# Between the output projection and the feed-forward network: reordering ScalarE, VectorE and GpSimd around the last token tile

## Chip, cores and metric

The kernel runs on one core of one Trainium2 chip. The metric is the device time of one execution, in microseconds (us). Engines are named as in the profile: PE is TensorE, DVE is VectorE, ACT is ScalarE, POOL is GpSimd, SP is SyncE, which here only issues transfers.

## The reference, cut to what matters

One layer of a hybrid diffusion backbone over 1024 tokens of width 1024. The change touches only the seam between its two halves:

```python
    m = (g[:, :, 0] * (ya @ w_branch[0]) + g[:, :, 1] * (yb @ w_branch[1])
         + g[:, :, 2] * (yc @ w_branch[2]))
    return m @ w_out
...
        x = x + mod_x[2] * rms_norm(mix, norm_g[l, 1])
        h2 = modulate(x, norm_g[l, 2], mod_x[3], mod_x[4])
        x = x + mod_x[5] * rms_norm(swiglu(h2, w_ffn_in[l], w_ffn_out[l]), norm_g[l, 3])
```

## The kernel before

All large products are taken in three passes over operands cut in two: a high part in the format of the fast float32 product (a copy to fp32r) and a low part (the value minus its high part). `parts_product` (L78 to L80) multiplies high by high, high by low and low by high, so every operand must be cut first. ScalarE makes high parts, GpSimd or VectorE the low ones; a low part reads two tensors in SBUF.

`residual_ffn_in` does two things. First, for each of 8 tiles t of 128 tokens (the last is t = 7, `LAST`), the output projection of the merged branches, then the residual and the second norm. PE accumulates the tile in two banks of PSUM. ACT takes its sum of squares (`square`), DVE the mean, ACT the root, DVE the reciprocal and the product with gate row and root (L2657, `o_xn`), which frees the banks (`taken`), and adds it to x (L2660, `x_ready`). ACT takes the sum of squares of x (`square_x`), DVE scales it (L2668, `xn_ready`), PE turns the tile (`turn`, 8 transposes), and `modulate` applies scale and shift out of PSUM into `h2`, on ACT, for the last tile half on ACT and half on DVE (L2693).

Second, the input projection of the feed-forward network over 22 pairs of gate and up weights, as a block scheme with 7 products (0 to 6) per pair in place of 8, of 12 matmuls each. It needs sums of blocks: on the side of `h2` the `half_sums` (T1 and T3, two subtractions of 128x512 for a token tile), T2 (`second_sum`), T4 (`fourth_sum`); on the side of the weights `s13` (two sums), `s2` and `s4`. All of these read two tensors in SBUF. In the profile T1 and T3 parts are `m_parts`, T2, B22 and T4 parts `i_t_hi` and `i_t_lo`, the first half's parts `b_hi` and `b_lo`, weights and their parts `stage`, `i_raw`, `i_s` and `i_hi`, `i_lo`, `cut_hi`, `cut_lo`.

The seam is the stretch in which the last tile's chain meets the first pair's products. Nothing schedules it but the order written out by hand: each engine works through its list in order and waits at semaphores. PE's list there is: tile 7's projection, turn of tile 6, product (0,0) (product 0 of pair 0), product (3,0) into the same bank, turn of tile 7, product (0,1) of the next pair, then (1,0), (2,0), (4,0), (6,0), (5,0) and from there the pairs' regular steps from (1,1) on. Product (3,0) waits for ACT's copy of the bank (`t1_ready`, L2429), which itself waits for `taken`. Product (0,1) waits for its weight's low part by POOL (`weight_lo(1, 1, 0)`). Product (1,0) waits for T1's low part, (4,0) for T2's, and (1,1) for the next pair's sum `s13(1, 1)` (L2618, L2620) with its high and low part.

## Time and profile before

| | us |
|---|---|
| median of 3 runs | 1778.73 (1776.87 to 1779.0) |
| the profiled execution | 1778.41 |
| its span | 1776.4 |
| PE busy | 1737.5 (98%) |
| DVE busy | 1222.7 (69%) |
| ACT busy | 804.2 (45%) |
| POOL busy | 766.7 (43%) |

The profiled execution is 2.0 us longer than its span, since the span begins with the first instruction and ends with the last. The seam lies at 1120 to 1170 us of it. A share of busy time is an average over the whole kernel: in the seam PE waits, and there DVE's list is full.

### The profile page before, as it was taken

What the parts mean: (1) busy time and instruction counts of PE and PEld (TensorE: products, weight loads), DVE (VectorE), ACT (ScalarE), POOL (GpSimd) and SP (SyncE); (2) the same over time, 40 slices, a digit from 0 to 9 for tenths busy, and PEclk for the clock granted to TensorE, in tenths of its full rate; (3) what the DMA queues carried; (4) which work ended last, traced back from release to release, by engine and by line L of the source; (5) the groups of instructions that cost most, each with busy time, mean ns of one, the idle gap of its engine ahead of it and who ended that gap; (6) DMA issues with size and microseconds to landing.
All of it is one profiled execution on the core that took longest, in us unless ns stands there. A gap on an engine that the chain in (4) does not pass through costs nothing. (4 is left out here: it accounts for less than half of the span.)

```text
span 1776.4 us, 25757 instructions
## 1 busy us (share of the span) xinstructions
PE 1737.5 (98%) x9180; PEld 1479.4 (83%) x9180; DVE 1222.7 (69%) x1719; ACT 804.2 (45%) x1576; POOL 766.7 (43%) x494
## 2 busy tenths in 40 slices
...
GB/s 329 106 103 123 115 119 143 156 153 182 265 172 210 170 146 137 151 33 72 1 143 160 89 166 84 83 106 120 94 94 127 121 94 128 114 278 208 253 102 177
DMA packets 98375, 249.86 MB, mean 141 GB/s; under 512 B 12257, under 2 KB 25953, under 8 KB 98146
## 3 DMA queue, kind: packets, MB, share of 16 engines
...
## 5 line engine op out<-in xcount | busy, mean ns | idle before, releaser
L736 POOL TENSOR_TENSOR ring<-raw_w,ring 128x512 fp32r<-128x512 f32 x120 | 186.9, 1575 | 139.9 <-ACT ring L607 139.8
L78 PE MATMUL psum<-h_hi,ring 128*128 128x512 f32 x400 | 156.8, 392 | 3.0 <-ACT z L653 2.0
L80 PE MATMUL psum<-h_hi,ring 128*128 128x512 f32 x400 | 156.4, 391 | 0.0
L79 PE MATMUL psum<-h_lo,ring 128*128 128x512 f32 x400 | 156.2, 391 | 0.0
L78 PE MATMUL psum<-u_slot 128*128 128x512 f32 x308 | 120.5, 391 | 0.9 <-DVE u_slot L2933 0.7
L80 PE MATMUL psum<-u_slot 128*128 128x512 f32 x308 | 120.2, 390 | 0.0
L79 PE MATMUL psum<-u_slot 128*128 128x512 f32 x308 | 119.9, 389 | 0.0
L607 ACT ACTIVATE ring<-raw_w 128x512 fp32r<-128x512 f32 x120 | 72.5, 625 | 101.0 <-DVE raw_w L895 32.3
L1386 DVE TENSOR_REDUCE mx<-psum 128x1 f32<-128x1280 f32 x64 | 95.1, 1486 | 6.8 <-PE psum L1272 6.0
L1319 ACT ACTIVATE e<-psum,neg_m 128x1280 f32<-128x1280 f32 x64 | 85.0, 1328 | 31.2 <-DVE neg_m L1387 31.2
L2532 POOL TENSOR_TENSOR cut_lo<-i_raw,cut_hi 128x512 fp32r<-128x512 f32 x44 | 66.8, 1520 | 59.2 <-ACT cut_hi L2387 59.2
L78 PEld LDWEIGHTS psum<-h_hi,ring 128*128 128x128 f32 x400 | 75.5, 189 | 20.1 <-issue 4.0
L79 PEld LDWEIGHTS psum<-h_lo,ring 128*128 128x128 f32 x400 | 75.5, 189 | 15.7
L80 PEld LDWEIGHTS psum<-h_hi,ring 128*128 128x128 f32 x400 | 75.4, 189 | 15.8
L2532 POOL TENSOR_TENSOR cut_lo<-stage,cut_hi 128x512 fp32r<-128x512 f32 x40 | 59.9, 1498 | 64.0 <-ACT cut_hi L2387 64.0
L1271 PE MATMUL psum<-k_st,q_st 128*128 128x512 f32 (+1 forms) x192 | 74.2, 387 | 5.6 <-ACT e L1319 4.6
L1285 PE MATMUL psum<-val,at 128*128 128x128 f32 x640 | 76.7, 275 | 0.0
L1285 PEld LDWEIGHTS psum<-val,at 128*128 128x128 f32 x640 | 74.0, 192 | 0.0
L78 PE MATMUL psum<-b_hi,cut_hi 128*128 128x512 f32 x176 | 69.5, 395 | 4.4 <-ACT gate_row L2429 2.0
L78 PE MATMUL psum<-m_parts,i_hi 128*128 128x512 f32 x176 | 69.5, 395 | 1.1 <-issue 0.8
L1723 ACT ACTIVATE we<-psum,wneg_m 128x640 f32<-128x640 f32 (+1 forms) x64 | 49.1, 768 | 46.8 <-DVE wneg_m L1835 44.0
L78 PE MATMUL psum<-i_t_hi,cut_hi 128*128 128x512 f32 x176 | 68.6, 390 | 1.3 <-POOL i_lo L2532 1.3
...
## 6 DMA issues: line engine op xcount, KB each, us to landing
...
```

The source lines that it names most:

```text
L78: pe.matmul(out, sh, mh, start=first, stop=False, skip_group_check=onto)
L79: pe.matmul(out, sh, ml, start=False, stop=False, skip_group_check=onto)
L80: return pe.matmul(out, sl, mh, start=False, stop=last, skip_group_check=onto)
L607: act.activation(w_hi[i], source(p, i), ACT.Copy).then_inc(w_hi_ready, 1)
L736: pool.tensor_tensor(w_lo[i], source(p, i), w_hi[i].bitcast(F32), ALU.subtract).then_inc(w_lo_ready, 1)
L1271: pe.matmul(out, q, k_st[j][:, s, c0:c0 + w], start=True, stop=False)
L1285: mm = pe.matmul(bank[:, 2 * P:3 * P], at[t % 2][:, k, :], val[t // TL % 2][:, k, :], start=(k == 0), stop=(k == TT - 1))
L1319: act.activation(e[i % 2][s][:], psum[:, 3 * s * HALF:3 * s * HALF + TOK], ACT.Exp, scale=SCALE, bias=neg_m[:, i % 2, s:s + 1], accum_out= ...
L1386: ch.link(v.tensor_reduce(mx[:, s:s + 1], psum[:, 3 * s * HALF:3 * s * HALF + TOK], AX.X, ALU.max))
L1723: act.activation(e[u % 2][s][:, 0:keys], psum[:, 2 * s * HALF + CTX:2 * s * HALF + CTX + keys], ACT.Exp, scale=SCALE, bias=neg_m[:, u % 2, ...
L2532: pool.tensor_tensor(f_lo[i], source(q, i), f_hi[i].bitcast(F32), ALU.subtract).then_inc(fw_lo_ready, 1)
```

## The change

Only the seam is edited.

- ACT: the root of tile 7 comes behind two conversions of tile 6; the high parts of weights 4 and 5 come later; the conversions of tile 7 come directly behind those of tile 6; T1 and T3 of tiles 6 and 7 are cut together, 128x4x256 in place of two of 128x4x128.
- DVE: for tile 7 the product with the gate row (L2668 of the changed kernel) is taken before the root is waited for, and frees the banks; root and residual then make one instruction (L2674). `s2` goes behind `o_xn`, `s4` behind T4's sum; the low parts of weights 6, 4 and 5 leave, those of 1 and 2 go behind x. T1 and T3 sums and low parts of tiles 6 and 7 are one instruction of 128x4x256 each.
- POOL: it no longer waits for three low parts of weights before its two T1 and T3 low parts of tile 5 (`m_parts`), no longer sums tile 6, and takes the low parts of weights 6, 4 and 5, the first once x of tile 7 is there.
- SP's next weight transfer waits for the split semaphores in place of one.

```diff
@@ -2288,24 +2292,25 @@
             mm = product(0, 1)
-            pe.wait_ge(w0_lo, w0_at(1))
-            pe.wait_ge(part_lo, 2 * FH - 1)
+            pe.wait_ge(*w0_lo_of[1])
+            pe.wait_ge(part_lo, 5)
             pe.wait_ge(taken, TL)
             product(1, 0).then_inc(prod0, 1)
-            pe.wait_ge(w0_lo, w0_at(2))
-            pe.wait_ge(part_lo, 2 * FH)
+            pe.wait_ge(*w0_lo_of[2])
+            pe.wait_ge(part_lo, 6)
             product(2, 0).then_inc(prod0, 1)
-            pe.wait_ge(w0_lo, w0_at(4))
+            pe.wait_ge(*w0_lo_of[4])
             pe.wait_ge(t_lo_ready[T2], 1)
             product(4, 0, lambda k: pe.wait_ge(t2b_lo_ready, k // 2 + 1)).then_inc(prod0, 1)
             pe.sem_inc(prod_done, PRODUCTS + 1)
-            pe.wait_ge(full_ready, KC * TL)
+            pe.wait_ge(full_ready, KC * LAST + KC // 2)
+            pe.wait_ge(last_full, KC // 2)
...
-            def square(t):
                                accum_out=ss[:, t % 2, 0:1]).then_inc(ss_ready, 1)
+                between()
                 act.wait_ge(mean_ready, 2 * t + 1)
                 act.activation(rs[:, t % 2, 0:1], ss[:, t % 2, 0:1], ACT.Sqrt).then_inc(root_ready, 1)
@@ -2420,10 +2426,8 @@
             first_weight_hi(6)
             first_weight_hi(1)
             first_weight_hi(2)
-            square(LAST)
-            first_weight_hi(4)
-            first_weight_hi(5)
-            modulate(LAST - 1, 0, 5)
+            square(LAST, lambda: modulate(LAST - 1, 0, 2))
+            modulate(LAST - 1, 2, 5)
             act.wait_ge(prod0, prod0_at(0))
             act.wait_ge(taken, TL)
             act.activation(t1, banks[0], ACT.Copy).then_inc(t1_ready, 1)
@@ -2431,10 +2435,14 @@
             act.sem_inc(fw_hi_ready, PRODUCTS)
             weight_hi(1, 1, 0)
             modulate(LAST - 1, 5, KC)
-            t1_hi(LAST - 1)
+            modulate(LAST, 0, KC // 2)
+            act.wait_ge(last_sums, 1)
+            act.activation(t1_part[0][:, :, two_first], h2[:, 0:KH, two_first], ACT.Copy).then_inc(part_hi, 1)
+            act.wait_ge(last_sums, 2)
+            act.activation(t3_part[0][:, :, two_first], h2[:, 0:KH, two_second], ACT.Copy).then_inc(part_hi, 1)
+            first_weight_hi(4)
             act.wait_ge(t2_sum, 2)
             t_part_hi(T2, slice(0, KH), slice(0, HALF // 2))
...
@@ -2484,11 +2492,9 @@
                 weight_hi(p + 1, q + 1, 6)
 
             every, far = slice(0, KH), slice(HALF // 2, HALF)
-            modulate(LAST, 0, KC // 2)
-            t1_hi(LAST)
-            t3_hi(LAST)
             act.wait_ge(t2_sum, 3)
             t_part_hi(T2, every, far)
+            first_weight_hi(5)
             t_part_hi(B22, slice(0, 2), slice(0, HALF))
@@ -2523,9 +2529,6 @@
                 pool.wait_ge(sums_done, 2 * (t - FH) + 1)
                 pool.wait_ge(full_ready, KC * (t + 1))
                 nc.gpsimd.tensor_tensor(h2[:, 0:KH, b], h2[:, KH:KC, b], h2[:, 0:KH, b], ALU.subtract).then_inc(sums_done, 1)
-                if t == LAST - 1:
-                    pool.sem_inc(fw_lo_ready, PRODUCTS)
-                    weight_lo(1, 1, 0)
 
...
             half_sums(FH + 1)
-            pool.wait_ge(w0_lo, 3)
             pool.tensor_tensor(src[T2][:, :, near], h2[:, KH:KC, beyond], src[T2][:, :, near], ALU.subtract).then_inc(t2_sum, 1)
-            half_sums(FH + 2)
             pool.wait_ge(t2_sum, 2)
             pool.wait_ge(t4_sum, 1)
             pool.tensor_tensor(src[T4][:, :, near], src[T4][:, :, near], src[T2][:, :, near], ALU.subtract).then_inc(t4_sum, 1)
+            def first_weight_lo(i):
+                pool.wait_ge(w0_hi, w0_at(i))
+                pool.tensor_tensor(f_lo[i], source(0, i), f_hi[i].bitcast(F32), ALU.subtract).then_inc(w0_lo_pool, 1)
+
+            pool.wait_ge(chunk_done, 4)
+            pool.wait_ge(x_ready, TL)
+            first_weight_lo(6)
+            pool.sem_inc(fw_lo_ready, PRODUCTS)
+            weight_lo(1, 1, 0)
+            first_weight_lo(4)
+            first_weight_lo(5)
             for i in range(1, PRODUCTS):
...
@@ -2604,13 +2616,14 @@
 
             def first_weight_lo(i):
                 v.wait_ge(w0_hi, w0_at(i))
-                v.tensor_tensor(f_lo[i], source(0, i), f_hi[i].bitcast(F32), ALU.subtract).then_inc(w0_lo, 1)
+                v.tensor_tensor(f_lo[i], source(0, i), f_hi[i].bitcast(F32), ALU.subtract).then_inc(w0_lo_dve, 1)
 
             def s13(p, q):
                 gate, up = raw[q % 2]
                 v.wait_ge(i_in[q % 2], (p - q % 2) * 16 + 32)
                 if q == 1:
-                    v.wait_ge(w0_lo, w0_at(2))
+                    v.wait_ge(w0_lo_pool, 3)
+                    v.wait_ge(*w0_lo_of[2])
@@ -2649,17 +2662,24 @@
                 root = lambda i: rs[:, t % 2, i:i + 1]
                 v.wait_ge(ss_ready, 2 * t + 1)
                 v.tensor_scalar(ss[:, t % 2, 0:1], ss[:, t % 2, 0:1], 1.0 / D, EPS, ALU.mult, ALU.add).then_inc(mean_ready, 1)
+                if t:
+                    v.wait_ge(turned, t)
+                if t == LAST:
+                    ch.link(v.tensor_tensor(xn[:], acc, row[:], ALU.mult))
+                    v.sem_inc(taken, 1)
                 v.wait_ge(root_ready, 2 * t + 1)
                 ch.link(v.reciprocal(root(0), root(0)))
-                if t:
-                    v.wait_ge(turned, t)
-
-                ch.link(v.scalar_tensor_tensor(out=xn[:], in0=acc, scalar=root(0), in1=row[:], op0=ALU.mult, op1=ALU.mult))
-                v.sem_inc(taken, 1)
                 v.wait_ge(x_in[t % 2], 16 * (t // 2 + 1))
-                v.tensor_tensor(x[t % 2][:], x[t % 2][:], xn[:], ALU.add).then_inc(x_ready, 1)
                 if t == LAST:
-                    first_weight_lo(4)
+                    v.scalar_tensor_tensor(out=x[t % 2][:], in0=xn[:], scalar=root(0), in1=x[t % 2][:], op0=ALU.mult,
+                                           op1=ALU.add).then_inc(x_ready, 1)
+                    v.wait_ge(chunk_done, 4)
+                    first_weight_lo(1)
+                    first_weight_lo(2)
+                else:
+                    ch.link(v.scalar_tensor_tensor(out=xn[:], in0=acc, scalar=root(0), in1=row[:], op0=ALU.mult, op1=ALU.mult))
+                    v.sem_inc(taken, 1)
+                    v.tensor_tensor(x[t % 2][:], x[t % 2][:], xn[:], ALU.add).then_inc(x_ready, 1)
                 v.wait_ge(ss_ready, 2 * t + 2)
                 v.tensor_scalar(ss[:, t % 2, 1:2], ss[:, t % 2, 1:2], 1.0 / D, EPS, ALU.mult, ALU.add).then_inc(mean_ready, 1)
                 v.wait_ge(root_ready, 2 * t + 2)
@@ -2667,16 +2687,11 @@
                 v.wait_ge(x_ready, t + 1)
                 v.tensor_scalar(xn[:], x[t % 2][:], root(1), None, ALU.mult).then_inc(xn_ready, 1)
                 if t == LAST:
-                    first_weight_lo(5)
+                    s2(0, 0)
                 if 1 <= t <= FH:
                     h_parts(t - 1)
                 if t == LAST - 1:
                     s13(0, 0)
-                    s2(0, 0)
-                    s4(0, 0)
-                    v.wait_ge(chunk_done, 4)
-                    for i in W0[:3]:
-                        first_weight_lo(i)
                 if t == FH + 1:
                     for n in range(2):
 
             far, beyond = slice(HALF // 2, HALF), slice(SEQ - HALF // 2, SEQ)
-            v.wait_ge(part_lo, 4)
-            part_lower(LAST - 1, 0)
             v.wait_ge(turned, TL)
             for k in range(KC // 2, KC):
                 v.tensor_scalar(h2[:, k, LAST * P:TL * P], turned_x(LAST, k), A2[:, k:k + 1], B2[:, k:k + 1], ALU.mult,
-                                ALU.add).then_inc(full_ready, 1)
-            a, b = first_half(LAST), second_half(LAST)
-            v.wait_ge(full_ready, KC * TL)
-            v.wait_ge(sums_done, 2 * (FH - 1))
-            v.tensor_tensor(h2[:, 0:KH, a], h2[:, 0:KH, b], h2[:, 0:KH, a], ALU.subtract).then_inc(sums_done, 1)
-            v.wait_ge(sums_done, 2 * FH - 1)
-            v.tensor_tensor(h2[:, 0:KH, b], h2[:, KH:KC, b], h2[:, 0:KH, b], ALU.subtract).then_inc(sums_done, 1)
-            part_lower(LAST - 1, 1)
-            part_lower(LAST, 0)
-            part_lower(LAST, 1)
-            v.wait_ge(part_lo, 2 * FH - 1)
+                                ALU.add).then_inc(last_full, 1)
+            v.wait_ge(full_ready, KC * LAST + KC // 2)
+            v.wait_ge(last_full, KC // 2)
+            v.tensor_tensor(h2[:, 0:KH, two_first], h2[:, 0:KH, two_second], h2[:, 0:KH, two_first], ALU.subtract).then_inc(last_sums, 1)
+            v.wait_ge(last_sums, 1)
+            v.tensor_tensor(h2[:, 0:KH, two_second], h2[:, KH:KC, two_second], h2[:, 0:KH, two_second], ALU.subtract)\
+             .then_inc(last_sums, 1)
+            v.wait_ge(part_lo, 4)
+            for n, (part, whole) in enumerate(((t1_part, two_first), (t3_part, two_second))):
+                v.wait_ge(part_hi, 5 + n)
+                v.tensor_tensor(part[1][:, :, two_first], h2[:, 0:KH, whole], part[0][:, :, two_first].bitcast(F32), ALU.subtract)\
+                 .then_inc(part_lo, 1)
+            v.wait_ge(part_lo, 5)
             v.wait_ge(t2_sum, 2)
             second_sum(far, beyond, FH)
             v.wait_ge(t4_sum, 2)
             fourth_sum(far, FH - 1)
+            s4(0, 0)
             t_part_lo(T2, slice(0, KH), slice(0, HALF // 2), 1, t_lo_ready[T2])
             for n in range(2):
```

VectorE from behind tile 6's `o_xn` to tile 7's second mean, before the change (`stage` and `i_s` are weights and their sums, `o_ss` the sums of squares):

```order
L2618 TENSOR_TENSOR i_s<-stage 128x512
L2620 TENSOR_TENSOR stage<-stage 128x512
L2629 TENSOR_TENSOR stage<-stage 128x512
L2636 TENSOR_TENSOR stage<-stage 128x512
L2607 TENSOR_TENSOR i_lo<-stage,i_hi 128x512 x2
L2607 TENSOR_TENSOR i_lo<-i_s,i_hi 128x512
L2651 TENSOR_SCALAR o_ss<-o_ss 128x1
L2653 RECIPROCAL o_rs<-o_rs 128x1
L2657 SCALAR_TENSOR_TENSOR o_xn<-psum,o_rs,gate_row 128x1024
L2660 TENSOR_TENSOR o_x<-o_x,o_xn 128x1024
L2607 TENSOR_TENSOR cut_lo<-stage,cut_hi 128x512
L2664 TENSOR_SCALAR o_ss<-o_ss 128x1
```

and after it:

```order
L2631 TENSOR_TENSOR i_s<-stage 128x512
L2633 TENSOR_TENSOR stage<-stage 128x512
L2664 TENSOR_SCALAR o_ss<-o_ss 128x1
L2668 TENSOR_TENSOR o_xn<-psum,gate_row 128x1024
L2671 RECIPROCAL o_rs<-o_rs 128x1
L2674 SCALAR_TENSOR_TENSOR o_x<-o_xn,o_rs,o_x 128x1024
L2619 TENSOR_TENSOR i_lo<-stage,i_hi 128x512
L2619 TENSOR_TENSOR i_lo<-i_s,i_hi 128x512
L2684 TENSOR_SCALAR o_ss<-o_ss 128x1
```

The sums `s2` and `s4` and the low part of weight 6 have left the place ahead of the first mean, and the low parts of weights 1 and 2 have come between x and the second mean in place of that of weight 4.

VectorE from tile 7's `o_xn` to the first low part of T2, before:

```order
L2668 TENSOR_SCALAR o_xn<-o_x,o_rs 128x1024
L2607 TENSOR_TENSOR cut_lo<-stage,cut_hi 128x512
L2596 TENSOR_TENSOR m_parts<-h,m_parts 128x4x128
L2693 TENSOR_SCALAR h<-psum,A,B 128x128 x4
L2698 TENSOR_TENSOR h<-h 128x4x128
L2700 TENSOR_TENSOR h<-h 128x4x128
L2596 TENSOR_TENSOR m_parts<-h,m_parts 128x4x128 x3
L2599 TENSOR_TENSOR h<-h 128x4x256
L2603 TENSOR_TENSOR h<-h 128x4x256
L2710 TENSOR_TENSOR i_t_lo<-h,i_t_hi 128x4x256
```

and after:

```order
L2688 TENSOR_SCALAR o_xn<-o_x,o_rs 128x1024
L2642 TENSOR_TENSOR stage<-stage 128x512
L2706 TENSOR_SCALAR h<-psum,A,B 128x128 x4
L2710 TENSOR_TENSOR h<-h 128x4x256
L2712 TENSOR_TENSOR h<-h 128x4x256
L2717 TENSOR_TENSOR m_parts<-h,m_parts 128x4x256 x2
L2611 TENSOR_TENSOR h<-h 128x4x256
L2615 TENSOR_TENSOR h<-h 128x4x256
L2649 TENSOR_TENSOR stage<-stage 128x512
L2725 TENSOR_TENSOR i_t_lo<-h,i_t_hi 128x4x256
L2725 TENSOR_TENSOR i_t_lo<-h,i_t_hi 128x2x256 x2
```

Behind the four conversions `h<-psum,A,B` stand seven wide instructions and `s4` (the second `stage<-stage`) where five of 128x4x128 and three wide ones stood, counting up to the first low part of T2.

GpSimd from tile 5's sums to the first low part of the next pair's sums, before:

```order
L2522 TENSOR_TENSOR h<-h 128x4x128
L2525 TENSOR_TENSOR h<-h 128x4x128
L2568 TENSOR_TENSOR m_parts<-h,m_parts 128x4x128 x2
L2573 TENSOR_TENSOR h<-h 128x4x128
L2522 TENSOR_TENSOR h<-h 128x4x128
L2525 TENSOR_TENSOR h<-h 128x4x128
L2532 TENSOR_TENSOR cut_lo<-i_raw,cut_hi 128x512
L2577 TENSOR_TENSOR h<-h 128x4x128
L2532 TENSOR_TENSOR i_lo<-i_raw,i_hi 128x512
```

and after:

```order
L2528 TENSOR_TENSOR h<-h 128x4x128
L2531 TENSOR_TENSOR h<-h 128x4x128
L2570 TENSOR_TENSOR m_parts<-h,m_parts 128x4x128 x2
L2575 TENSOR_TENSOR h<-h 128x4x128
L2578 TENSOR_TENSOR h<-h 128x4x128
L2581 TENSOR_TENSOR i_lo<-stage,i_hi 128x512
L2535 TENSOR_TENSOR cut_lo<-i_raw,cut_hi 128x512
L2581 TENSOR_TENSOR cut_lo<-stage,cut_hi 128x512 x2
L2535 TENSOR_TENSOR i_lo<-i_raw,i_hi 128x512
```

The two sums of tile 6 are gone from it, and three low parts of weights of the first pair have come, two of them behind the low part of the next pair's weight 0.

## Rows read from the trace of the kernel before

**Rows 1.** The page of the profile: span, and the busy time of TensorE.
```profile
span 1776.4 us, 25757 instructions
PE 1737.5 (98%) x9180; PEld 1479.4 (83%) x9180; DVE 1222.7 (69%) x1719; ACT 804.2 (45%) x1576; POOL 766.7 (43%) x494
```

**Rows 2.** The timeline of PE at the seam: start us, us, what, idle before.
```profile
1127.17 0.39 PE L80 MATMUL psum<-b_hi,cut_lo 128*128 128x512 f32 x1
1129.61 0.50 PE L78 MATMUL psum<-b_hi,cut_hi 128*128 128x512 f32 x1 [2.05 <-ACT gate_row L2429]
...
1134.02 1.06 PE L2244 MATMUL psum<-ident,o_xn 128*128 128x128 f32 x8
1136.73 0.50 PE L78 MATMUL psum<-b_hi,cut_hi 128*128 128x512 f32 x1 [1.65 <-POOL cut_lo L2532]
...
1140.50 0.47 PE L78 MATMUL psum<-m_parts,i_hi 128*128 128x512 f32 x1 [0.77 <-issue]
...
1146.18 0.39 PE L78 MATMUL psum<-i_t_hi,cut_hi 128*128 128x512 f32 x1
...
1154.83 0.48 PE L78 MATMUL psum<-m_parts,i_hi 128*128 128x512 f32 x1 [0.30 <-POOL i_lo L2532]
...
1168.37 0.47 PE L78 MATMUL psum<-i_t_hi,cut_hi 128*128 128x512 f32 x1 [1.28 <-POOL i_lo L2532]
```

**Rows 3.** Stretches: us, busy PE PEld DVE ACT POOL, PE clock, DMA share, GB/s.
```profile
1130.50:1134.50 4.00, 4.00 (x15) 3.11 (x14) 3.45 (x6) 3.39 (x9) 3.08 (x3) 0.57 0.32 131
```

**Rows 4.** The timeline of VectorE (DVE) at the seam, columns as in Rows 2.
```profile
1121.97 0.69 DVE L2620 TENSOR_TENSOR stage<-stage 128x512 f32<-128x512 f32 x1
...
1126.51 1.28 DVE L2657 SCALAR_TENSOR_TENSOR o_xn<-psum,o_rs,gate_row 128x1024 f32<-128x1024 f32 x1
1127.94 1.93 DVE L2660 TENSOR_TENSOR o_x<-o_x,o_xn 128x1024 f32<-128x1024 f32 x1
1129.80 1.78 DVE L2607 TENSOR_TENSOR cut_lo<-stage,cut_hi 128x512 fp32r<-128x512 f32 x1
1131.50 0.14 DVE L2664 TENSOR_SCALAR o_ss<-o_ss 128x1 f32<-128x1 f32 x1
...
1132.11 1.16 DVE L2668 TENSOR_SCALAR o_xn<-o_x,o_rs 128x1024 f32<-128x1024 f32 x1
...
1135.48 1.36 DVE L2693 TENSOR_SCALAR h<-psum,A,B 128x128 f32<-128x128 f32 x4
1137.10 1.38 DVE L2698 TENSOR_TENSOR h<-h 128x512 f32<-128x512 f32 x1 [0.26 <-ACT h L2354]
...
1140.92 1.22 DVE L2599 TENSOR_TENSOR h<-h 128x1024 f32<-128x1024 f32 x1
...
1143.38 3.62 DVE L2710 TENSOR_TENSOR i_t_lo<-h,i_t_hi 128x1024 fp32r<-128x1024 f32 x5
...
1151.14 0.68 DVE L2618 TENSOR_TENSOR i_s<-i_raw 128x512 f32<-128x512 f32 x1
```

**Rows 5.** Groups of VectorE: line, shapes, count, busy us, mean ns, idle.
```profile
L3149 DVE SCALAR_TENSOR_TENSOR u_high<-u_high,u_ss,u_x 128x1024 f32<-128x1024 f32 x4 | 5.1, 1285 | 0.1
```

**Rows 6.** The timeline of GpSimd (POOL) at the seam, columns as in Rows 2.
```profile
1119.49 1.29 POOL L2525 TENSOR_TENSOR h<-h 128x512 f32<-128x512 f32 x1
1126.06 2.73 POOL L2568 TENSOR_TENSOR m_parts<-h,m_parts 128x512 fp32r<-128x512 f32 x2 [5.28 <-DVE i_lo L2607]
1128.73 2.30 POOL L2573 TENSOR_TENSOR h<-h 128x512 f32<-128x512 f32 x1
1130.99 1.73 POOL L2522 TENSOR_TENSOR h<-h 128x512 f32<-128x512 f32 x1
...
1136.64 1.28 POOL L2577 TENSOR_TENSOR h<-h 128x512 f32<-128x512 f32 x1
```

**Rows 7.** The timeline of ScalarE (ACT) before the last tile's square.
```profile
1122.69 0.64 ACT L2375 ACTIVATE i_hi<-stage 128x512 fp32r<-128x512 f32 x1 [0.72 <-DVE stage L2620]
...
1123.99 1.02 ACT L2339 ACTIVATE o_junk<-psum 128x1024 bf16<-128x1024 f32 x1
```

More of the change, by code:

```diff
@@ L2119, in residual_ffn_in @@
             sem(f"fi_{n}") for n in ("w_hi", "w_lo", "s", "acc", "t1", "p5", "z", "u2", "x", "silu", "f", "dve"))
-        w0_hi, w0_lo, prod0 = sem("fi_w0_hi"), sem("fi_w0_lo"), sem("fi_acc0")
+        w0_hi, w0_lo_pool, w0_lo_dve, prod0 = sem("fi_w0_hi"), sem("fi_w0_lo_pool"), sem("fi_w0_lo_dve"), sem("fi_acc0")
+        last_full, last_sums = sem("fi_last_full"), sem("fi_last_sums")
         W0 = (6, 1, 2, 4, 5)
@@ L2123, in residual_ffn_in @@
         w0_at = lambda i: W0.index(i) + 1
+        w0_lo_of = {1: (w0_lo_dve, 1), 2: (w0_lo_dve, 2), 6: (w0_lo_pool, 1), 4: (w0_lo_pool, 2), 5: (w0_lo_pool, 3)}
+        two_first, two_second = slice(HALF // 2, HALF), slice(SEQ - HALF // 2, SEQ)
         prod0_at = lambda i: ORDER0.index(i) + 1
@@ L2201, in step @@
                     sp.wait_ge(m_lo_ready, TL + 1)
-                    sp.wait_ge(w0_lo, len(W0))
+                    sp.wait_ge(w0_lo_pool, 3)
+                    sp.wait_ge(w0_lo_dve, 2)
                 for j in range(2):
@@ L2290, in _ @@
             mm = product(0, 1)
-            pe.wait_ge(w0_lo, w0_at(1))
-            pe.wait_ge(part_lo, 2 * FH - 1)
+            pe.wait_ge(*w0_lo_of[1])
+            pe.wait_ge(part_lo, 5)
             pe.wait_ge(taken, TL)
             product(1, 0).then_inc(prod0, 1)
-            pe.wait_ge(w0_lo, w0_at(2))
-            pe.wait_ge(part_lo, 2 * FH)
+            pe.wait_ge(*w0_lo_of[2])
+            pe.wait_ge(part_lo, 6)
             product(2, 0).then_inc(prod0, 1)
-            pe.wait_ge(w0_lo, w0_at(4))
+            pe.wait_ge(*w0_lo_of[4])
             pe.wait_ge(t_lo_ready[T2], 1)
             product(4, 0, lambda k: pe.wait_ge(t2b_lo_ready, k // 2 + 1)).then_inc(prod0, 1)
-            pe.wait_ge(w0_lo, w0_at(6))
+            pe.wait_ge(*w0_lo_of[6])
             pe.wait_ge(z_ready, 1)
             product(6, 0, lambda k: pe.wait_ge(t_lo_ready[T4], k + 1)).then_inc(prod0, 1)
-            pe.wait_ge(w0_lo, w0_at(5))
+            pe.wait_ge(*w0_lo_of[5])
             product(5, 0, lambda k: pe.wait_ge(t_lo_ready[B22], k + 1)).then_inc(prod0, 1)
@@ L2333, in cut_m, with square @@
                 act.activation(m_hi[t % 2][:], m[:, :, t * P:(t + 1) * P], ACT.Copy).then_inc(m_hi_ready, 1)
-            def square(t):
+            def square(t, between=lambda: None):
                 act.wait_ge(acc_done, t + 1)
@@ L2433, in _ @@
             modulate(LAST - 1, 5, KC)
-            t1_hi(LAST - 1)
+            modulate(LAST, 0, KC // 2)
[4 more added lines that the diff above has]
+            first_weight_hi(4)
             act.wait_ge(t2_sum, 2)
             t_part_hi(T2, slice(0, KH), slice(0, HALF // 2))
-            t3_hi(LAST - 1)
             def first_product(p, q):
@@ L2806, in _ @@
             s4(1, 1)
-            v.wait_ge(part_lo, 2 * FH)
+            v.wait_ge(part_lo, 6)
             finish(0, 0, Chain(v, fdve, 0))
```

## The prediction

> **What bounds the kernel now.** I read the page first: TensorE is busy for 1737.5 of 1776.4 us [rows 1], so an edit outside its list can give back only its idle time. Its timeline at the seam shows where that lies: 2.05 us ahead of product (3,0), 1.65 ahead of (0,1), 0.77 ahead of (1,0), and behind the seam still 0.30 ahead of (1,1) at 1154.83 and 1.28 at 1168.37 [rows 2]. After the first of these waits comes a stretch at a mean granted clock of 0.57, which is for the most part the lower level of 1.2 GHz in place of 2.4 [rows 3].
>
> The other engines' timelines show what these waits hang on. The late ones decide: (1,1) waits for the next pair's sums, and VectorE reaches these at 1151.14 after a list that runs with hardly a hole from 1135.48 on [rows 4]. Whatever is gained ahead of that list arrives at the regular steps only if VectorE also gets to 1151.14 earlier. So I follow one chain: the last tile through VectorE to the sum s13(1,1). What its start moves, the kernel's end moves. The steps behind (2,0) have slack only on TensorE: it starts (4,0) at 1146.18, while the low part it needs is done at 1145.20.
>
> **How VectorE and GpSimd meet.** Instructions with two tensors in SBUF don't run together. VectorE's addition to x takes 1.93 us where a free one of this shape takes 1.22 (1140.92), and it ends at 1129.87, 1.08 behind GpSimd's m_parts pair, which ends at 1128.79. GpSimd's next (1128.73) ends 1.15 behind that, VectorE's next (1129.80) 0.55 behind this, GpSimd's next 1.14 behind that: they take turns, and each waits for the whole instruction of the other [rows 4, 6]. VectorE's instruction out of PSUM at 1126.51 ran beside m_parts in its usual 1.28, and the one-input one at 1132.11 beside L2522. My rules: a blocked 512 instruction of VectorE ends 0.55 behind GpSimd's, a blocked 1024 one 1.08 behind, and GpSimd's 1.15 behind VectorE's. Free ones follow each other every 0.60 (512) or 1.14 (1024), some 0.1 more where one waits for the other's semaphore.
>
> The Trainium skill has this rule (SBUF — State Buffer, section "Who interferes with whom"): a VectorE instruction with two SBUF inputs and a GpSimd instruction that reads SBUF exclude each other for the whole instruction, and the one issued second fully blocks. The rows could also be read as a mere slowdown, 1.78 for every 512 instruction; by that s13 would end some 0.4 us later than by the lock, and the sum below would be 0.4 higher. The end times of the four neighbours agree with the page's rule.
>
> **The change, step by step.** Times in us of the profile of before.
>
> 1. GpSimd ends its last sum of tile 5 at 1120.78 [rows 6]. It no longer waits for VectorE's low parts, so its first m_parts runs 1120.8 to 1122.1, into VectorE's s13, which before ran free to 1122.66 [rows 4]. First sum blocked: 1122.1 + 0.55 = 1122.7. Second m_parts: 1123.8. Second sum: 1124.35, 1.7 late.
> 2. ScalarE's high part of weight 1 needs that sum, and its square of tile 7 stands two high parts (0.54 each) behind. Before, they started at 1122.69 and 1123.99 [rows 7]. Now: 1124.4 + 1.1 = 1125.5, 1.5 late, though the tile has been in PSUM since 1124.
> 3. From the square's start to its sum 1.1 (1126.6), mean 0.15, product with the gate row 1.28 [rows 4]: the banks are free at 1128.05. The root, behind two conversions, is ready by then. Reciprocal with its semaphores 0.2, then the fused instruction, priced as the last ones of the kernel, 1.285 [rows 5]: x at 1129.5. Before: 1129.87. Of 1.9 us taken off this piece 1.5 went in step 2.
> 4. ScalarE copies the bank at about 1128.4 to 1129.0, behind its conversions and the free bank. Product (3,0) starts at 1129.0 in place of 1129.61, a wait of 1.45.
> 5. At x the low parts of weights 1 and 2 (VectorE) meet that of 6 (GpSimd): 1130.05, then GpSimd 1131.2, then 1131.75. The second mean stands behind them: 1131.65 in place of 1131.50. From its start to xn's end 1.77 as before [rows 4]: 1133.4. Turn: 1.06 [rows 2], 1134.55, TensorE waiting some 1.6 ahead of it. Before, (3,0) on the slow clock had held it to 1134.02 to 1135.08, and VectorE began its conversions only at 1135.48. It now begins at 1134.6, **0.9 ahead**. s2 fits in (it ends 0.55 behind GpSimd's weight 0, near 1134.5), and (0,1) follows the turn without a wait.
> 6. Conversions to first sum 1.6 [rows 4]: 1136.2. Two wide sums of 1.22: 1138.65. First wide low part: 1139.8, and (1,0) starts there, 0.7 ahead of 1140.50. TensorE waits 2.4 us, since (0,1) is done at 1137.4.
> 7. Second low part 1140.95. By then ScalarE has made weight 4's high part, and GpSimd's low part cuts in to 1142.1. T2 1143.2, T4 1144.45, s4 1145.1, T2's near low part 1146.25. s4 frees ScalarE for weight 5, GpSimd cuts in again to 1147.4, T2's first far low part 1147.95. Before: 1145.20, the second of the five instructions at 1143.38. Product (4,0) starts at 1148.0 in place of 1146.18; the wait for it is 2.6.
> 8. From there the list is the same: s13(1,1) starts 5.94 later (1145.20 to 1151.14 before), at 1153.9 in place of 1151.14. Product (1,1) starts at 1157.6 in place of 1154.83, and TensorE, done with (5,0) at about 1156.3, waits for it. The gap at 1168.37 hangs on the same chain and moves along.
>
> The sum, on VectorE from conversions to s13(1,1): 15.66 before. Added: s4 0.6, two wide sums for two narrow 1.05, two wide low parts for three narrow 0.5 (before, 1.8 ahead of 1140.92), two turns of GpSimd 2.2 less the 0.7 that its L2577 cost before (1136.64, [rows 6]); together 3.65. Less the earlier start of 0.9: **+2.75 us** (by step 8's own times 2.76).
>
> The edit of SP's wait costs nothing: the next weights are asked for when GpSimd's weight 5 is done, near 1147.4, 21 us ahead of the wait at 1168.37, the first that hangs on them. The clock: a slow stretch in (3,0) is covered by the wait for xn, one in (1,0) and (2,0) by the wait for (4,0); one in (4,0) to (5,0) costs up to 2 of which 1.3 are covered, the rest by the wait at the following product.
>
> **The rivals.**
> - *The early collisions don't come* (steps 1 and 5): GpSimd's two m_parts miss s13, since it runs some 1.5 us later or earlier than I lay it. Then xn is ready near 1131.1, the turn ends near 1132.2, and with the late collisions the sum is +0.4: 1779.1. For it: a shift of GpSimd by little more than one of its own instructions (1.29) would do. Against: 1120.78 is a row, and the program has nothing between.
> - *No turn taking at all*: then also the late 2.2 fall away, and the sum is -1.8: 1776.9. The rows speak against it; even so the gain is small, because VectorE's list grew.
> - *TensorE's idle time is what counts* (the other sign): the waits of 2.05, 1.65 and 0.77 shrink and stay gained, 4 us: 1774.7. That needs s13(1,1) at 1147 and so a turn before 1130.5, which x alone at 1129.5 excludes.
> - *Heavier* (slower by over 0.2%): the slow stretch falls onto the turn, with transposes at half the clock and the end of (3,0) past 1133.4. The turn then ends 1 to 1.6 later, the sum is 3.8 to 4.3: 1782.8. It decides if the turn ends behind 1135.4. Before, the clock fell 1 us after a wait of 2.05; now the wait is 1.45, with a second of 1.6 close behind.
>
> **How the numbers follow.** The profiled execution took 1778.41, 0.3 under the median; the sum is the same against both. Median 1778.73 + 2.7 = 1781.4, profiled execution 1781.1, span 1779.1. Chances: forecast 0.60 (own range 1780.3 to 1782.6), early collisions missing 0.13, no turns 0.04, idle time gained 0.03, heavier 0.20. The range 1778.9 to 1783.3 leaves out the two gains, a little of the missing-collision case and the end of the heavy one. 0.2% is 3.56 us, about what a measurement of this kernel can tell from no change: slower means above 1782.3. That is the heavy case and a tenth of the forecast's: 0.27. Faster, below 1775.2: 0.04. Within: 0.69.
>
> **What would show it.** Steps 1 and 2: m_parts on GpSimd near 1121, s13 in 1.4 and 1.6 us instead of 0.69, the square near 1125.5. Step 5: the two low parts on VectorE in about 2.4 us. Steps 6 and 7: idle TensorE of about 2.4 ahead of (1,0) and 2.6 ahead of (4,0), with T2 on VectorE at about 2.3 us for 1.22. Step 8: s13(1,1) near 1153.9. I am wrong if s13(1,1) starts at or before 1151, or if the regular steps start earlier than VectorE's list moved.

## The result and the profile after

| | median us | lowest to highest | runs |
|---|---|---|---|
| before, same chip | 1778.55 | 1775.31 to 1781.55 | 22 |
| changed | 1781.44 | 1778.0 to 1784.5 | 22 |

The ratio is 1.0018 with a 95% interval of 1.0012 to 1.0024: 2.1 to 4.3 us slower. The forecast was 1781.4, and "within 0.2%" was the likeliest of the three outcomes. Two executions are left out of the experiments' ratios below, since the chip ran in a slow state in them: one of x7 (4505.01 us) and one of the kernel before (9548.59 us).

The page of the changed kernel, lines as in [rows 1]:

```profile
span 1781.5 us, 25758 instructions
PE 1739.5 (98%) x9180; PEld 1481.2 (83%) x9180; DVE 1220.1 (68%) x1714; ACT 804.6 (45%) x1574; POOL 769.2 (43%) x495
```

The span is 5.1 us longer than in [rows 1], more than the medians differ. The timeline of TensorE splits it. The first row below is tile 6's turn, the last step that the change leaves alone (1123.79 in the trace of before, `L2244`, 8 transposes); the last is the regular wait of 1168.37 in [rows 2].

```profile
1125.56 1.03 PE L2248 MATMUL psum<-ident,o_xn 128*128 128x128 f32 x8
1131.08 0.50 PE L78 MATMUL psum<-b_hi,cut_hi 128*128 128x512 f32 x1 [1.76 <-ACT gate_row L2433]
...
1135.31 1.09 PE L2248 MATMUL psum<-ident,o_xn 128*128 128x128 f32 x8 [1.17 <-DVE o_xn L2688]
...
1142.06 0.47 PE L78 MATMUL psum<-m_parts,i_hi 128*128 128x512 f32 x1 [2.61 <-issue]
...
1150.26 0.47 PE L78 MATMUL psum<-i_t_hi,cut_hi 128*128 128x512 f32 x1 [2.36 <-DVE i_t_lo L2725]
...
1160.64 0.47 PE L78 MATMUL psum<-m_parts,i_hi 128*128 128x512 f32 x1 [0.30 <-PE psum L80]
...
1173.30 0.47 PE L78 MATMUL psum<-i_t_hi,cut_hi 128*128 128x512 f32 x1 [1.30 <-POOL i_lo L2535]
```

Tile 6's turn already comes 1.77 later, though TensorE's list is the same up to there, and GpSimd's last sum of tile 5, which the change leaves alone too, is later by as much (1121.25 for 1119.49). In the other twelve traces it lies anywhere from 1121.72 to 1125.84, so this part is the execution's and not the change's. From that turn to the last row it is 1173.30 - 1125.56 = 47.74 us, against 1168.37 - 1123.79 = 44.58 before: **+3.16 us in the seam**. Another 0.2 lie behind it. From here on every seam is measured from its own tile 6's turn, and for times on the scale of the prediction 1.77 is taken off the rows of after.

The waits of TensorE ahead of (3,0), (0,1) and (1,0) were 2.05, 1.65 and 0.77, together 4.47 [rows 2]. Now there are 1.76 ahead of (3,0), 1.17 ahead of the turn, 2.61 ahead of (1,0) and 2.36 ahead of (4,0): 7.90.

VectorE, the chain that the prediction followed:

```profile
1121.86 1.23 DVE L2688 TENSOR_SCALAR o_xn<-o_x,o_rs 128x1024 f32<-128x1024 f32 x1
1123.02 1.79 DVE L2631 TENSOR_TENSOR i_s<-stage 128x512 f32<-128x512 f32 x1
1124.84 1.68 DVE L2633 TENSOR_TENSOR stage<-stage 128x512 f32<-128x512 f32 x1
...
1130.37 1.28 DVE L2674 SCALAR_TENSOR_TENSOR o_x<-o_xn,o_rs,o_x 128x1024 f32<-128x1024 f32 x1
1131.57 0.69 DVE L2619 TENSOR_TENSOR i_lo<-stage,i_hi 128x512 fp32r<-128x512 f32 x1
1132.17 1.80 DVE L2619 TENSOR_TENSOR i_lo<-i_s,i_hi 128x512 fp32r<-128x512 f32 x1
1133.89 0.14 DVE L2684 TENSOR_SCALAR o_ss<-o_ss 128x1 f32<-128x1 f32 x1
...
1134.50 0.75 DVE L2688 TENSOR_SCALAR o_xn<-o_x,o_rs 128x1024 f32<-128x1024 f32 x1
1135.17 1.76 DVE L2642 TENSOR_TENSOR stage<-stage 128x512 f32<-128x512 f32 x1
1136.85 1.35 DVE L2706 TENSOR_SCALAR h<-psum,A,B 128x128 f32<-128x128 f32 x4
...
1143.06 2.31 DVE L2611 TENSOR_TENSOR h<-h 128x1024 f32<-128x1024 f32 x1
...
1147.22 4.69 DVE L2725 TENSOR_TENSOR i_t_lo<-h,i_t_hi 128x1024 fp32r<-128x1024 f32 x5
...
1156.05 0.68 DVE L2631 TENSOR_TENSOR i_s<-i_raw 128x512 f32<-128x512 f32 x1
```

And GpSimd beside it:

```profile
1121.25 1.30 POOL L2531 TENSOR_TENSOR h<-h 128x512 f32<-128x512 f32 x1
1122.50 3.47 POOL L2570 TENSOR_TENSOR m_parts<-h,m_parts 128x512 fp32r<-128x512 f32 x2
...
1131.79 1.63 POOL L2581 TENSOR_TENSOR i_lo<-stage,i_hi 128x512 fp32r<-128x512 f32 x1 [2.74 <-issue]
1134.92 1.46 POOL L2535 TENSOR_TENSOR cut_lo<-i_raw,cut_hi 128x512 fp32r<-128x512 f32 x1 [1.50 <-ACT cut_hi L2393]
1142.48 1.81 POOL L2581 TENSOR_TENSOR cut_lo<-stage,cut_hi 128x512 fp32r<-128x512 f32 x1 [6.10 <-ACT cut_hi L2381]
1148.05 1.51 POOL L2581 TENSOR_TENSOR cut_lo<-stage,cut_hi 128x512 fp32r<-128x512 f32 x1 [3.75 <-ACT cut_hi L2381]
```

The two lists are read side by side, by ends. GpSimd's first `m_parts` (to 1124.25) holds up the first sum of `s13` and its second (to 1125.97) lies between the two sums: they take 1.79 and 1.68 us in place of 0.69. Its low part of weight 6 (to 1133.42) makes VectorE's second low part 1.80 (to 1133.97). That of weight 0 (to 1136.38) makes `s2` 1.76 (to 1136.93). Weight 4 (to 1144.29) makes T2's sum 2.31 (to 1145.37), and weight 5 (to 1149.56) lies in the five low parts, 4.69 where [rows 4] has 3.62. A VectorE instruction that loses the turn doesn't show as idle time: it shows as one that takes longer, and ends 0.55 (128x512) or 1.08 (128x1024) behind GpSimd's.

### The profile page after: what moved, and what is told of

Read it like the earlier page. It is cut to its first block and busy times, and to the rows that moved or that the text cites. A ratio compares the mean times of both kernels' runs of the same rounds, so it can differ in the third digit from the quotient of the medians.

```text
span 1781.5 us, 25758 instructions
## 1 busy us (share of the span) xinstructions
PE 1739.5 (98%) x9180; PEld 1481.2 (83%) x9180; DVE 1220.1 (68%) x1714; ACT 804.6 (45%) x1574; POOL 769.2 (43%) x495
```

## The experiments

Each seam is measured from the start of its tile 6's turn to the late TensorE row with the wait of about 1.3 us (1.0 in the last three) at the end of the list above, and set against the 44.58 of before. There is one trace for each kernel; the pairs whose lists are the same up to the B22 low parts (before and x10, changed and x11, x6 and x9) start their conversions within 0.01 us of each other, so this comparison inside a trace shows some hundredths. The times, 9 to 12 runs each and spread over some 6 us, show about 2. Columns: us from the turn to the end of x, of tile 7's `o_xn`, to the start of its conversions on VectorE, of (4,0), of `s13(1, 1)` and of (1,1); then the seam against before, and the ratio of times.

| kernel | x | xn | conversions | (4,0) | s13(1,1) | (1,1) | seam | ratio, 95% |
|---|---|---|---|---|---|---|---|---|
| before | 6.09 | 9.48 | 11.69 | 22.39 | 27.35 | 31.03 | 0 | |
| changed | 6.09 | 9.70 | 11.29 | 24.70 | 30.49 | 35.08 | +3.16 | 1.0018, 1.0012 to 1.0024 |
| x1 | 4.26 | 8.93 | 10.54 | 23.97 | 29.77 | 33.34 | +2.37 | 1.0011, 1.0001 to 1.002 |
| x2 | 6.10 | 8.70 | 10.30 | 23.72 | 29.51 | 33.09 | +2.12 | 1.001, 1.0001 to 1.002 |
| x3 | 6.09 | 9.68 | 11.29 | 23.70 | 29.32 | 32.91 | +1.96 | 1.0009, 1.0 to 1.0018 |
| x4 | 6.08 | 9.46 | 11.68 | 22.37 | 27.33 | 31.02 | -0.02 | 1.0002, 0.9993 to 1.0011 |
| x5 | 5.38 | 7.97 | 9.57 | 22.00 | 27.62 | 31.19 | +0.23 | 1.0001, 0.9992 to 1.001 |
| x6 | 4.43 | 7.02 | 8.39 | 20.67 | 26.46 | 30.03 | -0.92 | 0.9999, 0.999 to 1.0007 |
| x7 | 6.08 | 9.47 | 11.69 | 27.05 | 31.56 | 35.69 | +4.28 | 1.0023, 1.0014 to 1.0033 |
| x8 | 6.09 | 9.48 | 11.69 | 22.39 | 27.35 | 31.04 | +0.07 | 1.0002, 0.9993 to 1.0011 |
| x9 | 4.43 | 7.03 | 8.39 | 21.82 | 24.05 | 31.39 | -0.91 | 0.9998, 0.9989 to 1.0007 |
| x10 | 6.08 | 9.46 | 11.68 | 22.37 | 24.93 | 32.26 | -0.04 | 1.0004, 0.9995 to 1.0013 |
| x11 | 6.11 | 9.70 | 11.30 | 24.73 | 28.12 | 35.44 | +3.13 | 1.0015, 1.0006 to 1.0024 |

The theory is the prediction's: VectorE's instructions with two inputs in SBUF and GpSimd's take turns, and the seam grows by VectorE's longer list and by the turns that it gives up. The first rival is that TensorE's own work or its clock makes the time; the second, that only the longer list does, and GpSimd is not in it.

**x1: the early collision taken away.** In the changed kernel GpSimd's `m_parts` wait for VectorE's two sums.

```diff
             half_sums(FH + 1)
+            pool.wait_ge(s_ready, 2)
             for n, part, whole in ((0, t1_part, first_half), (1, t3_part, second_half)):
```

> The changed kernel with one wait put back in another form: GpSimd starts tile 5's two low parts (m_parts) only when both sums of s13 are done. Theory (VectorE and GpSimd take turns, and VectorE's list from the last tile to the next pair's s13 sets the end): s13 takes 0.7 us each in place of 1.79 and 1.68, ScalarE's square of tile 7 starts when the tile is in PSUM, and x is ready 0.75 to 1.9 us earlier, depending on whether GpSimd's fourth instruction gets in ahead of it; the time is 1.0 to 2.2 above the kernel before in place of 2.9. Rival (TensorE's waits and its clock make the loss, or the growth of VectorE's list behind the turn alone): no effect, 2.9 above.

VectorE in x1:

```profile
1122.13 0.68 DVE L2632 TENSOR_TENSOR i_s<-stage 128x512 f32<-128x512 f32 x1
1122.85 0.69 DVE L2634 TENSOR_TENSOR stage<-stage 128x512 f32<-128x512 f32 x1
...
1128.85 1.78 DVE L2620 TENSOR_TENSOR i_lo<-stage,i_hi 128x512 fp32r<-128x512 f32 x1
1130.55 1.77 DVE L2620 TENSOR_TENSOR i_lo<-i_s,i_hi 128x512 fp32r<-128x512 f32 x1
```

The sums are back at 0.68 and 0.69, the square starts 1.86 earlier and x ends 1.83 earlier. But GpSimd is now late with T4's sum, and this and weight 6 block both low parts behind x. Of 1.83 us 0.77 arrive at xn and 0.79 at the seam's end.

**x2: weight 6 out of the way of the second mean.** GpSimd takes its low part behind that of the next pair's weight 0.

```diff
-            first_weight_lo(6)
             pool.sem_inc(fw_lo_ready, PRODUCTS)
             weight_lo(1, 1, 0)
+            first_weight_lo(6)
```

> The changed kernel with GpSimd's low part of weight 6 behind that of the next pair's weight 0, so that it no longer meets VectorE's low parts of weights 1 and 2 ahead of the second mean. Theory: the second low part on VectorE takes 0.7 in place of 1.80, the second mean stands 1.0 us earlier, weight 6's low part falls beside conversions out of PSUM, which don't need a turn; the time is 1.9 above the kernel before (0.9 to 2.3). Rival (this stretch is hidden by TensorE's product (3,0) and its turn): 2.9 above.

VectorE in x2, behind x:

```profile
1129.53 0.68 DVE L2619 TENSOR_TENSOR i_lo<-stage,i_hi 128x512 fp32r<-128x512 f32 x1
1130.14 0.68 DVE L2619 TENSOR_TENSOR i_lo<-i_s,i_hi 128x512 fp32r<-128x512 f32 x1
1130.84 0.15 DVE L2684 TENSOR_SCALAR o_ss<-o_ss 128x1 f32<-128x1 f32 x1
```

Both low parts are free, xn ends 1.00 earlier, and the seam gets back 1.04.

**x3: weights 4 and 5 back on VectorE.** Their low parts stand behind T2's sum and T2's near low part; the semaphores are adapted.

```diff
-            first_weight_lo(4)
-            first_weight_lo(5)
...
             second_sum(far, beyond, FH)
+            first_weight_lo(4)
...
             t_part_lo(T2, slice(0, KH), slice(0, HALF // 2), 1, t_lo_ready[T2])
+            first_weight_lo(5)
```

> The changed kernel with the low parts of weights 4 and 5 on VectorE, at the places in its list where GpSimd's cut in. Theory: two turns of GpSimd of 1.1 us are replaced by two own instructions of 0.6, so 1.0 less: 1.9 above the kernel before (1.5 to 2.4), although VectorE has two instructions more. Rival (VectorE's own busy time counts, GpSimd runs beside it): 1.2 more than the changed kernel, 4.1 above.

VectorE in x3:

```profile
1141.47 1.22 DVE L2609 TENSOR_TENSOR h<-h 128x1024 f32<-128x1024 f32 x1
1142.60 0.69 DVE L2617 TENSOR_TENSOR cut_lo<-stage,cut_hi 128x512 fp32r<-128x512 f32 x1
```

Doing the two instructions itself costs VectorE 0.60 each; leaving them to GpSimd cost it 1.1 to 1.2 each. `s13(1, 1)` comes 1.17 earlier, the seam gets back 1.20: the work that the change moved off VectorE made VectorE's list longer. The second rival, for which two more instructions on VectorE could only cost, fails here.

**x5: the three together.** The edits of x1, x2 and x3 in one kernel.

> The changed kernel with three edits together: GpSimd's m_parts wait for s13, weight 6's low part comes behind the next pair's weight 0, weights 4 and 5 are cut on VectorE. Theory: the parts add, 0.75 to 1.9 and 1.0 and 1.0 off 2.9: from 1.0 below to 0.2 above the kernel before. Rival (only the growth of the list behind the turn counts): 2 to 3 above.

The seam gets back 2.93 of 3.16 (0.79, 1.04 and 1.20 are 3.03), and the time is that of before. What the change adds to VectorE's list otherwise is about paid for by the earlier start of its conversions, 9.57 in place of 11.69. Two collisions are left ahead of them: that of `s2` (1.77 us for 0.69), and that of x, whose fused instruction meets T4's sum (GpSimd, to 1126.08) and takes 2.40 us for 1.28.

**x4: the gate product alone.** In the kernel before, only tile 7's gate product goes ahead of the root, with the fused instruction behind it.

```diff
+                if t:
+                    v.wait_ge(turned, t)
+                if t == LAST:
+                    ch.link(v.tensor_tensor(xn[:], acc, row[:], ALU.mult))
+                    v.sem_inc(taken, 1)
                 v.wait_ge(root_ready, 2 * t + 1)
...
                 if t == LAST:
+                    v.scalar_tensor_tensor(out=x[t % 2][:], in0=xn[:], scalar=root(0), in1=x[t % 2][:], op0=ALU.mult,
+                                           op1=ALU.add).then_inc(x_ready, 1)
                     first_weight_lo(4)
```

> The kernel before with one part of the change alone: for tile 7 the product with the gate row ahead of the root, and root and residual in one instruction. Theory: the banks are free 0.5 us earlier, but ScalarE is busy until 1128.9 anyway, and the fused instruction is blocked by GpSimd's m_parts until 1128.8 as the addition was, so x stays at 1129.9: 0 (within 0.5) against the kernel before. Rival (this part makes the gain that the rest of the change loses): 0.7 to 1.5 below it. Other rival (the fused instruction itself costs): 0.5 to 1 above.

VectorE and, in the next fence, GpSimd in x4:

```profile
1125.49 2.35 DVE L2661 SCALAR_TENSOR_TENSOR o_x<-o_xn,o_rs,o_x 128x1024 f32<-128x1024 f32 x1
```

```profile
1124.03 2.73 POOL L2568 TENSOR_TENSOR m_parts<-h,m_parts 128x512 fp32r<-128x512 f32 x2 [5.28 <-DVE i_lo L2607]
```

The fused instruction takes 2.35 for 1.28: it could start earlier, but waits out GpSimd's pair (to 1126.76) and ends 1.08 behind it, where the addition to x ended before. x stands at 6.08 for 6.09. As long as GpSimd holds that place, the gate product moves nothing.

**x7 and x8: the disputed cost by itself.** In the kernel before, GpSimd gets four instructions of 128x512 behind T4's sum, into a buffer that nobody reads then: in x7 subtractions, which read SBUF, in x8 memsets, which only write. They add work and change no output.

```diff
+            pool.wait_ge(full_ready, KC * TL)
+            for j in range(2):
+                pool.wait_ge(x_out[j], 16 * TL // 2)
+            for n in range(4):
+                pool.tensor_tensor(g[1][:], h2[:, KH, HALF:SEQ], h2[:, KH + 1, HALF:SEQ], ALU.subtract).then_inc(probe, 1)
+                pool.wait_ge(probe, n + 1)
```

In x8 the fifth line is:

```diff
+                pool.memset(g[1][:], 0.0).then_inc(probe, 1)
```

> The kernel before with four more GpSimd subtractions of 128x512 (two tensors in SBUF, into a buffer that nobody reads) in the 15 us in which GpSimd is idle and VectorE's list is full. Theory: each takes a turn of VectorE's, 1.1 us: s13(1,1) and the time 3.3 to 4.6 above the kernel before. Rival (GpSimd runs beside VectorE, its load costs nothing): 0.

> The same with four GpSimd memsets of the same 128x512 buffer, which read nothing in SBUF. Theory: VectorE's second input and GpSimd's read are what exclude each other, so an instruction that only writes costs VectorE nothing: 0 (within 0.5). Rival (any GpSimd instruction takes a turn): 2 to 4.6 above. The Trainium skill (SBUF - State Buffer, section Who interferes with whom) says the first.

GpSimd and VectorE in x7:

```profile
1139.93 6.78 POOL L2583 TENSOR_TENSOR i_g<-h 128x512 f32<-128x512 f32 x4
```

```profile
1140.55 1.67 DVE L2707 TENSOR_TENSOR h<-h 128x512 f32<-128x512 f32 x1
1142.14 5.12 DVE L2603 TENSOR_TENSOR m_parts<-h,m_parts 128x512 fp32r<-128x512 f32 x3
```

GpSimd and VectorE in x8:

```profile
1138.12 2.27 POOL L2583 MEMSET i_g<- 128x512 f32 x4
```

```profile
1138.76 0.69 DVE L2707 TENSOR_TENSOR h<-h 128x512 f32<-128x512 f32 x1
1139.37 1.89 DVE L2603 TENSOR_TENSOR m_parts<-h,m_parts 128x512 fp32r<-128x512 f32 x3
```

Four reading instructions make VectorE's next four 6.8 us long in place of 2.6, and the seam 4.28 longer: 1.07 each, and TensorE has not one instruction more. Four writing ones cost 0.07 in all. This is the one suspected cost by itself: GpSimd's reads alone lengthen the seam, with VectorE's and TensorE's lists untouched, which neither rival allows.

**x6: an order of my own.** From the changed kernel: `s13`, `s2`, `s4` and the low parts of weights 1 and 2 ahead of the first mean, those of 6, 4 and 5 on VectorE behind x, xn and T2's near low part; GpSimd takes its first `m_parts` behind VectorE's low part of weight 2, the second behind x, and the low part of the next pair's weight 0 behind xn. ScalarE makes weight 4's high part behind the root. The core of the edit:

```diff
             half_sums(FH + 1)
+            pool.wait_ge(w0_lo_dve, 2)
             for n, part, whole in ((0, t1_part, first_half), (1, t3_part, second_half)):
+                if n:
+                    pool.wait_ge(x_ready, TL)
...
+            pool.wait_ge(xn_ready, TL)
+            pool.sem_inc(fw_lo_ready, PRODUCTS)
+            weight_lo(1, 1, 0)
```

> An arrangement of my own out of both kernels: s13, s2, s4 and the low parts of weights 1 and 2 ahead of tile 7's first mean as before, gate product ahead of the root, all low parts of the first pair on VectorE, the others in its holes while it waits for the second mean and the turn; GpSimd does only one m_parts ahead of x and the next pair's weight 0 directly behind xn. By the rules of turns: x near 1128.1, VectorE's conversions from 1132.5, s13(1,1) near 1150.3 in place of 1151.1: 0.9 below the kernel before (2.0 below to 0.5 above). Rival (TensorE-bound, its waits fall by 3 us or more): 3 below or more.

TensorE in x6, the waits ahead of (3,0), (0,1) and (1,0):

```profile
1128.44 0.50 PE L78 MATMUL psum<-b_hi,cut_hi 128*128 128x512 f32 x1 [0.69 <-ACT gate_row L2433]
...
1132.79 0.51 PE L78 MATMUL psum<-b_hi,cut_hi 128*128 128x512 f32 x1 [0.45 <-POOL cut_lo L2534]
...
1138.60 0.47 PE L78 MATMUL psum<-m_parts,i_hi 128*128 128x512 f32 x1 [2.75 <-issue]
```

VectorE begins its conversions 3.30 earlier than before, and of these 0.89 arrive at `s13(1, 1)` and 0.92 at the seam's end. The wait ahead of (3,0) shrank from 2.05 to 0.69 and came back ahead of (1,0). In time it is 0.9999 of before, which can't be told from no change.

**x9, x10 and x11: is `s13(1, 1)` the bound?** In x6, before and changed in turn, it goes ahead of the four low parts of B22.

```diff
-            for k in range(KH):
-                t_part_lo(B22, k, slice(0, HALF), k // 2 + 1, t_lo_ready[B22])
             s13(1, 1)
+            for k in range(KH):
+                t_part_lo(B22, k, slice(0, HALF), k // 2 + 1, t_lo_ready[B22])
```

> My own arrangement (x6) with the next pair's two s13 sums ahead of B22's four low parts in VectorE's list, where nothing but the list holds them back. If s13(1,1) is what the regular steps wait for (step 8 of the prediction), they come up to 2.4 us earlier, until TensorE's own products (4,0), (6,0), (5,0) are the bound; GpSimd's low parts of the next weights then start among B22's low parts and take turns with them, which gives about 1 us back. Expected: 1.9 below the kernel before (3.0 to 0.5 below). Rival (the chain over T2's low part and (4,0) is the bound): as x6, 0.9 below or nearer to 0.

> The kernel before with this one edit: s13(1,1) ahead of B22's low parts. TensorE waited 0.30, 0.72 and 1.28 us behind the seam for what hangs on s13(1,1); these waits go, and GpSimd's turns among B22's low parts make (5,0) end about 1.1 later. Expected: 1.3 below the kernel before (2.2 below to 0). Rival (s13(1,1) does not bound): 0 to 1.1 above.

> The changed kernel with the same edit. If the 2.9 us of the change come in through s13(1,1), most of them go, until TensorE, which starts (4,0) 2.3 us later than before, is the bound: 0.5 to 1.5 above the kernel before. Rival (the loss comes in through (4,0) alone): 2.3 to 3 above.

VectorE and GpSimd in x10:

```profile
1146.65 0.68 DVE L2618 TENSOR_TENSOR i_s<-i_raw 128x512 f32<-128x512 f32 x1
...
1147.98 4.68 DVE L2710 TENSOR_TENSOR i_t_lo<-h,i_t_hi 128x512 fp32r<-128x512 f32 x4
...
1162.69 0.68 DVE L2618 TENSOR_TENSOR i_s<-stage 128x512 f32<-128x512 f32 x1
```

```profile
1148.81 1.61 POOL L2532 TENSOR_TENSOR i_lo<-i_raw,i_hi 128x512 fp32r<-128x512 f32 x1 [12.96 <-ACT i_hi L2387]
1150.38 1.74 POOL L2532 TENSOR_TENSOR i_lo<-i_s,i_hi 128x512 fp32r<-128x512 f32 x1
```

`s13(1, 1)` starts 2.4 us earlier in all three, but the gains that were expected don't come: the seam's end moves by 0.01, 0.04 and 0.03 us. Product (1,1) even starts later, by 1.36, 1.23 and 0.36. The sum's high parts are made sooner, so GpSimd's low parts come sooner, and now they take turns with B22's four low parts (4.68 us) and with `s2`, which stands behind these. In x10 `s2` ends 32.62 us behind tile 6's turn, in the kernel before 29.55. ScalarE in x10 waits for it:

```profile
1154.38 0.64 ACT L2387 ACTIVATE cut_hi<-i_raw 128x512 fp32r<-128x512 f32 x1 [4.61 <-DVE i_raw L2629]
1155.03 1.28 ACT L2463 ACT_TABLE_LOAD   x1
1156.33 0.60 ACT L2463 ACTIVATE i_g<-psum 128x512 f32<-128x512 f32 x1
1156.82 0.62 ACT L2387 ACTIVATE cut_hi<-i_raw 128x512 fp32r<-128x512 f32 x1
```

The last row is the high part of `s4`'s sum. `s4` itself ends 1.27 us earlier than before, but its high part stands behind that of `s2`, a table load and an activation, and starts 35.10 us behind the turn, where in the kernel before it is 35.13. From there on the two run alike; VectorE reaches the next pair's sum 1162.69 - 1121.72 = 40.97 us behind the turn, before 1164.80 - 1123.79 = 41.01. So the edit took one delay away and put another of the same size in its place. Behind the low parts of T2 the lists of the three kernels are the same, so this is one test made three times, and that the two delays are equal is not explained by it. What moving `s2` along would give was not run.

In the other runs the place of the next pair's sum moves as the seam's end does: 44.16 in the changed kernel (+3.15), 41.23 in x5 (+0.22), 40.09 in x6 (-0.92).

## Why the prediction was right, point by point

The time, the turn taking and the steps' order held; one start was mis-sized, and the rule in step 8 was put too widely. Times in brackets are the forecast's, on its scale.

- **Steps 1 and 2 held, 0.4 off.** Second sum to 1124.75 (1124.35), square at 1125.84 (1125.5). The 0.4 is that GpSimd's first `m_parts` was itself blocked: it ends 1.16 behind tile 6's scaling of xn (from 1123.09 to 1124.25 in the trace of after). I had taken this scaling, which reads one tensor, for free of turns. x1 shows both sides: without the collision the square comes at its old time.
- **Steps 3 and 4 held:** x to 1129.88 (1129.5; before 1129.87), (3,0) at 1129.3 (1129.0) behind a wait of 1.76 (1.45). x4 shows the other half of this: GpSimd had held x's place before as well.
- **Step 5 is where a size failed:** I had conversions start 0.9 ahead of before, they start 0.40 ahead. The second mean came 0.47 late, the scaling took 0.75 in place of 1.16 and gave most of this back (xn to 1133.49 for 1133.4), and the turn was over at 1134.63 (1134.55). But `s2` did not fit in. GpSimd's weight 0 ran until 1134.61, not 1134.0, and VectorE ended `s2` 0.55 behind it, so that the conversions started 0.45 behind the turn's end. In x6, where the instruction behind xn ran free, they start 0.04 behind it.
- **Steps 6 and 7 held,** all 0.5 later with their start: (1,0) at 1140.29 (1139.8) behind 2.61 (2.4), (4,0) at 1148.5 (1148.0) behind 2.36 (2.6). From conversions to `s13(1, 1)` it is 19.20 us against a forecast of 15.66 + 3.65 = 19.31. x3 gives the two cuts a size of 1.2 us beyond what VectorE would spend on the same work.
- **The sum:** +3.54 for the list less 0.40 for the start is +3.14; forecast was +3.65 less 0.9. The seam shows +3.16, and the medians 2.9. The terms add up here as they were laid, with the start mis-sized by 0.5. By the seam the sum was 0.4 short, so that the median came out 0.04 from 1781.4 is luck: its interval alone is 2 us wide.
- **Step 8's number held (`s13(1, 1)` at 1154.28 for 1153.9), its reason only in part.** Where the list from there on is left alone, the seam's end does move as `s13(1, 1)` does: by 3.16 and 3.14 in the changed kernel, and in x1 to x8 the two differ by 0.07 at most. But "What its start moves, the kernel's end moves" is wrong as a statement on that instruction alone: x9, x10 and x11 moved it by 2.4 us and the end by nothing, since the same edit made `s2` and ScalarE's steps behind it the late ones.
- **The rivals.** "No turn taking" falls with x7. "TensorE's idle time is what counts" falls with the changed kernel itself, where the waits went from 4.47 to 7.90 us, and with x6, where the waits ahead of (3,0) and (0,1) shrank by 2.56 us together and the end moved by 0.92. "Early collisions missing" is x1 and x2: the collisions were there, and taking them away gives back 0.79 and 1.04, which by difference leaves +1.3 where the rival had +0.4. That price let VectorE begin its conversions 3.25 ahead of before (3.65 less 0.4); x5, where those of x (2.40 for 1.28) and of `s2` remain, begins them 2.12 ahead.

**The slow clock did come, in (4,0) to (5,0).** The window of the changed kernel, columns as in [rows 3]:

```profile
1150.00:1156.00 6.00, 5.74 (x18) 4.62 (x19) 6.00 (x11) 2.42 (x4) 0.00 (x0) 0.72 0.50 175
```

The granted clock is 0.72 over these 6 us, between the levels of 1.2 and 2.4 GHz: 0.57 from 1151.56 to 1155.56, for the most part the lower one. It fell about 1.2 us after the wait of 2.36 was over (the matmuls of 0.39 become 0.52 at 1151.49 and 0.63 behind that). Product (1,1) starts 4.05 later than before, 0.9 more than `s13(1, 1)` asks, and what released it is TensorE's own `psum`. At the seam's end this 0.9 is gone: the waits behind took it, as the prediction had it for this place. The rival with the slow stretch on the turn didn't occur (8 transposes in 1.09 us).

Nor does the clock make the seam's length. x11 has its slow stretch elsewhere, at a granted clock of 0.72 from 16 to 22 us behind tile 6's turn, where the changed kernel has 1.00, and its seam is +3.13 for +3.16. x6 has 1.00 over the whole seam, and x9, with 0.57 over 4 us of it, ends within 0.01 of x6.

Of the rule that the prediction weighed in the Trainium skill (SBUF — State Buffer, section "Who interferes with whom"), x7 and x8 show both halves: a GpSimd instruction that reads SBUF excludes VectorE's two-input ones (1.07 us each), one that only writes doesn't (0.07 for four). What is left open: why the two delays in x9, x10 and x11 are equal, and whether a version exists that is surely faster than before. x6 gains 0.92 us in the trace, a twentieth of a per cent, and its time can't show that.
